# Exchanging the score products and the turning of probabilities in each step of a streamed attention loop

## What is computed

```python
def sink_attention(q, k, v, bias, mask, sink):          # branch A: own chunk and the two before it
    s = jnp.einsum('nqkgd,nskd->nkgqs', q, k).astype(jnp.float32) * SCALE + bias
    s = jnp.where(mask, s, NEG)
    m = jnp.maximum(jnp.max(s, axis=-1, keepdims=True), sk)
    p = jnp.exp(s - m)
    p = p / (jnp.sum(p, axis=-1, keepdims=True) + jnp.exp(sk - m))
    return jnp.einsum('nkgqs,nskd->nqkgd', p.astype(v.dtype), v)

def fox_attend(q, k, v, cq, ck, q_pos, k_pos):          # branch B: causal, with forgetting
    s = jnp.einsum('bqhd,bshd->bhqs', q, k).astype(jnp.float32) * SCALE
    s = s + jnp.transpose(cq, (0, 2, 1))[..., :, None] - jnp.transpose(ck, (0, 2, 1))[..., None, :]
    s = jnp.where(k_pos[None, :] <= q_pos[:, None], s, NEG)
    p = jax.nn.softmax(s, axis=-1)
    return jnp.einsum('bhqs,bshd->bqhd', p.astype(v.dtype), v)
```

## Time and profile before

| | us |
|---|---|
| median of 3 runs | 1903.26 |
| lowest and highest | 1902.57, 1903.67 |
| the profiled execution | 1898.65 |
| its span, from first to last instruction | 1896.8 |
| TensorE products busy | 1742.3 (92%) |
| TensorE weight loads busy | 1572.7 (83%) |
| VectorE busy | 779.0 (41%) |
| ScalarE busy | 649.3 (34%) |

### The profile page before, as it was taken

The page is one execution under the profiler, slowest core; times in us unless marked ns, Lnnn a source line. Parts: engine busy times, 40 slices in busy tenths (PEclk is TensorE's granted clock), DMA queues, the critical chain, the costliest instruction groups (busy, mean ns, idle before and its releaser), DMA issues.

```text
span 1896.8 us, 27394 instructions
## 1 busy us (share of the span) xinstructions
PE 1742.3 (92%) x10220; PEld 1572.7 (83%) x10220; DVE 779.0 (41%) x1717; ACT 649.3 (34%) x1174; POOL 80.7 (4%) x147
## 2 busy tenths in 40 slices
PE   4999999999999888984999999998979999999994
PEld 3999999999999878763788887778759999997773
DVE  6625655555556333431322223445342222223333
ACT  5234444554445333321322223345222222222232
POOL 2101111000000010000000000000000000000000
PEclk9999999999999999997899999998988999999997
DMA  5243425443423546634233332236312222222221
GB/s 147 59 123 103 138 84 160 129 122 112 135 73 105 135 132 195 197 105 158 67 100 96 92 100 89 89 100 198 105 45 67 80 86 78 88 77 67 78 72 55
DMA packets 214663, 201.02 MB, mean 106 GB/s; under 512 B 13175, under 2 KB 175512, under 8 KB 214056
## 3 DMA queue, kind: packets, MB, share of 16 engines
q1 hardware_dynamic: 203664, 164.66, 29.9%
q0 software_dynamic: 10912, 35.19, 5.2%
HBM read 166.04 MB, written 33.83 MB: 105 GB/s over the span
## 4 chain that ended last, share of the span: by engine, by line
PE 88%; DVE 4%; DMA 3%; ACT 2%; issue 1%; SPq 1%; DVEq 0%; POOLq 0%; POOL 0%; ACTq 0%
PE ps L1462 25%; PE ps L1463 24%; PE ps L1464 24%; PE ps L1555 6%; PE ps L1515 4%; PE ps L1532 3%; DMA w_raw<-in_w_ob_dram 1%; DMA xa<-in_x_prompt_dram 1%; DVE x L1374 1%; PE ps L1567 1%; DVE h_lo L1070 1%; DVE yn L1064 1%; DMA w_raw<-in_w_gu_dram 1%; PE ps L1602 1%; ACT w_hi L754 0%
## 5 line engine op out<-in xcount | busy, mean ns | idle before, releaser
L1462 PE MATMUL ps<-h_hi,w_hi 128*128 128x288 f32 (+3 forms) x1872 | 620.3, 331 | 2.3 <-DVE h_lo L1070 2.3
L1464 PE MATMUL ps<-h_hi,w_lo 128*128 128x288 f32 (+3 forms) x1872 | 613.8, 328 | 0.0
L1463 PE MATMUL ps<-h_lo,w_hi 128*128 128x288 f32 (+3 forms) x1872 | 613.8, 328 | 0.0
L1051 DVE TENSOR_TENSOR w_lo<-w_raw,w_hi 128x1024 fp32r<-128x1024 f32 x198 | 242.3, 1224 | 708.5 <-ACT w_hi L754 708.4
L754 ACT CAST w_hi<-w_raw 128x1024 fp32r<-128x1024 f32 x198 | 208.2, 1051 | 719.1 <-PE ps L1464 665.3
L1462 PEld LDWEIGHTS ps<-h_hi,w_hi 128*128 128x128 f32 x1872 | 354.5, 189 | 17.5 <-DVE h_lo L1070 2.9
L1463 PEld LDWEIGHTS ps<-h_lo,w_hi 128*128 128x128 f32 x1872 | 354.5, 189 | 14.0 <-issue 0.2
L1464 PEld LDWEIGHTS ps<-h_hi,w_lo 128*128 128x128 f32 x1872 | 354.1, 189 | 14.0
L1462 PE MATMUL ps<-w_hi,as_hi 128*128 128x512 f32 (+1 forms) x396 | 157.9, 399 | 10.9 <-DVE as_lo L1426 6.9
L1463 PE MATMUL ps<-w_lo,as_hi 128*128 128x512 f32 (+1 forms) x396 | 156.9, 396 | 0.0
L1464 PE MATMUL ps<-w_hi,as_lo 128*128 128x512 f32 (+1 forms) x396 | 156.1, 394 | 0.0
(11 more groups left out here) (216 smaller groups left out, 2024.4 us busy)
## 6 DMA issues: line engine op xcount, KB each, us to landing
w_raw<-in_w_gu_dram SPq DMA_DIRECT2D x176, 256.0 KB, 3.2
w_raw<-in_w_down_dram SPq DMA_DIRECT2D x88, 256.0 KB, 2.8
w_raw<-in_w_in_dram SPq DMA_DIRECT2D x68, 256.0 KB, 3.4
zg_d<-stg POOLq DMA_DIRECT2D x28, 544.0 KB, 3.0
w_raw<-in_w_out_dram SPq DMA_DIRECT2D x32, 256.0 KB, 3.1
gate<-zg_d SPq DMA_DIRECT2D x8, 576.0 KB, 4.3
qz<-zg_d SPq DMA_DIRECT2D x16, 272.0 KB, 5.6
negc_s<-negc_d SPq DMA_DIRECT2D x8, 528.0 KB, 6.1
```

What stands on the lines that cost most here:

```text
L1051: nc.vector.tensor_tensor(w_lo[:, slot, :], w_raw[:, slot, :], w_hi[:, slot, :].bitcast(F32), ALU.subtract) \
L1462: nc.tensor.matmul(out, l_hi, r_hi, start=start, stop=False)
L1463: nc.tensor.matmul(out, l_hi, r_lo, start=False, stop=False)
L1464: return nc.tensor.matmul(out, l_lo, r_hi, start=False, stop=stop)
```

## The change

On TensorE alone, the first two blocks of a step change places. Before, a step turned the probabilities of unit n and then made the scores of unit n+2; after, the scores of unit n+2 come first. The programs of all other engines, and all waits inside the blocks, stay as they are.

```diff
             for n in range(N_STREAM):
-                turn(n)
                 if n + 2 < N_STREAM:
                     scores(n + 2)
+                turn(n)
                 for ev in turns_at[n]:
                     turn_one(ev)
                 p = piece_at(n)
```

## The result

The changed kernel takes 1917.45 us (median of 4 runs, 1915.36 to 1918.42) against 1903.38 us: 14.1 us more, a ratio of 1.0077 with a 95% interval of 1.0062 to 1.0092. (One more run of the kernel before, and the median of 1903.26 stands at 1903.38.) The direction was forecast, the size was not: 1911.7 was forecast, and 1917.45 lies above the range.

What follows compares the result with a forecast made beforehand. TensorE, busy almost throughout the attention loop, was taken as the bound. To 1903.26 us came 4.6 for late score banks and 3.8 for joins between blocks: 1911.7 us, range 1905.0 to 1915.5.

Steps and rivals of the forecast that it cites:

- The bound of the kernel: Attention loop: TensorE is busy almost throughout, with no wait for exponentials to fill, so nothing to win.
- An even step has a dense piece ... which hides everything: Even steps: about 4 us of dense work between turn(n) and outputs(n-1) hides every wait.
- The late bank, k = 4: Forgetting half, odd step with four key blocks: next scores wait 0.72 us for VectorE's fold; all such waits 4.6 us.
- k = 3, 5, 6: The same wait in odd steps with three, five or six key blocks: 0.27, 0.10 and 0.05 us per head pair.
- The seams: Joins between TensorE's blocks cost 0.04 us more in each of 95 steps: 3.8 us, bounds 1.0 and 7.6.
- In odd steps of the window half the idle stays, and covers the seam: TensorE's 0.25 us idle ahead of turn_one remains there and hides the cost of joining blocks.
- Nothing comes back: New units behind the loop: their waits follow TensorE's own progress, so what the loop loses, the end loses.
- no change: Rival: joins cost nothing and VectorE's signal comes 0.5 us sooner, so 1903.3 us; chance 0.25.
- The second chain: Rival: VectorE's later splits in odd steps delay o_tok, so outputs wait in 11 steps, 5.5 us, total 1917.2; chance 0.06.
- The clock rival: Rival: small idles pull the granted clock to 0.93 through 276 us, 21 us more, total 1932; chance 0.02.
- The faster case: Rival: the turn starts sooner behind the long scores, 0.05 us a step, 6.7 in all, total 1896.6; chance 0.05.

Runs made afterwards that it cites:

- e1: Scores and turn exchanged in even steps alone, against the kernel before: 1904.06 us, ratio 1.0010.
- e2: Scores and turn exchanged in odd steps alone, against the kernel before: 1910.80 us, ratio 1.0046.
- e4: Changed kernel, with VectorE taking ot_lo ahead of the fold in odd steps of the window half: 1907.90 us, ratio 1.0027 to the kernel before.

## Why the prediction was wrong, point by point

- **The bound of the kernel**: right. There was no wait of the turn to fill, and every form of the new order that was tried made the loop longer (e1 by 1.2 us, e2 by 7.4).
- **"An even step has a dense piece ... which hides everything"**: this step failed. It hides outputs(n-1), but turn_one stands ahead of the dense piece, and it waits for bank 7. So the sum put the window half's waits at nothing. VectorE's rows behind those of the earlier trace rows had the price: `ot_lo` through at 218.65 and turn_one at 218.71, which is the way back and no room, against a turn that comes about 0.3 us later. The runs showed 20 x 0.25 = 4.95 us in its place, gone with one move on VectorE (e4). With them the forecast would have been near 1917.
- **The late bank, k = 4**: right, 0.72 forecast, 0.75 measured; its term-by-term times stand in the trace. In one of the four pairs it cost 1.16. In that step the copy started 0.74 us after the last transposition, and not 0.38, in the kernel before too; the reason is open.
- **k = 3, 5, 6**: 0.27, 0.10, 0.05 forecast, 0.39, 0.14, 0.04 measured. The second piece for k = 3 was undersized by a third. All of it: 4.6 forecast, 5.7 measured, outside its bounds (the lower one, stated as 3.6, is 3.8 by its own terms: 4 x 0.94).
- **The seams**: 3.8 forecast, oversized. The odd steps with 3 to 8 blocks cost 0.045 each, as estimated, but those with two blocks nothing, and the even steps of the forgetting half nothing clear (-0.05 to 0.04 where no bank is late). The window half has 0.7 us outside the 20 steps. Together 1.9 us by the table.
- **"In odd steps of the window half the idle stays, and covers the seam"**: right, 0.005 us on average in each of 35.
- **Nothing comes back**: right for the waits. The 9.3 us at L1585 and 4.1 at L1532 in the new units are the same after.
- **The rivals**: no change falls. The second chain exists, but not where I looked: it goes through `ot_lo` and turn_one, not through `o_tok` and outputs. Its price was listed as 5.5 us, and the one that came was 4.9; that the two are near is luck. The clock rival falls in the loop (1.00). The faster case falls: short products behind a long one gained nothing.

Two errors of opposite sign partly cancelled (late bank 1.1 too small, seams 1.9 too large), by luck. The missed chain of 4.9 us is what put the time outside the range: without it 1917.45 would be 1912.5. The open 1.6 us behind the loop would not have sufficed to bring it in, 1915.9 against 1915.5.

## What to carry to other kernels

When a block of an in-order engine is moved later, list every buffer that its consumer gives back in the same program step, not only the one whose wait is moved. Here VectorE's step hands back three in a row (`probT`'s bank, a score bank, bank 7), and in the window half the third was the tight one. For each, take the distance from the giver's last instruction to the taker's first in the trace of before, less the distance that stands there when the taker really waits. Both were 0.06 us here, so the room was nothing. And where products overlap, measure a loop from one mark to the same mark; a list of idles showed 3.2 of 12.5 us here.

The Trainium skill ("Perfetto Trace Analysis", Optimization Strategy) says that a gap which repeats on the busiest engine can mean too few buffers. The step times agree: turn_one has one PSUM bank, and its 20 steps lost 4.95 us, the most after the score banks' 5.7. The list of idles shows 4 of the 20. e4 shows that it can also mean the wrong order on the engine that empties them.

## What was not expected of the hardware

A wait need not be seen to be paid: the steps behind k = 3 grew by 0.39 us, and the list of TensorE's waits has none for them. And the fold that starts without a VectorE instruction right ahead of it began 0.49 us after the last transposition, where a copy began at 0.39.
